# A two-block transformer on one core: moved roundings and taps beside a scan, and cross-attention scores in three rounded passes

## The reference, cut to what matters

```python
def mem_cross_attention(xn, mem, mem_g, wq, wk, wv, wo):   # 4 heads of 256, 512 tokens, 256 memory rows
...
    s = jnp.einsum('bshd,bmhd->bhsm', q, k).astype(jnp.float32) * (XATTN_HEAD_DIM ** -0.5)
    pr = jax.nn.softmax(s, axis=-1).astype(v.dtype)
    o = jnp.einsum('bhsm,bmhd->bshd', pr, v).reshape(B, S, D_MODEL)
    return o @ wo
...
def stick_breaking_attention(q, k, v):      # second block, 8 heads of 64, s < t
        z = jnp.einsum("bqhd,bkhd->bhqk", qb, kb) * scale
        log_beta = jax.nn.log_sigmoid(z)
        log_one_minus = jnp.where(mask, jax.nn.log_sigmoid(-z), 0.0)
        tail = lax.cumsum(log_one_minus, axis=3, reverse=True) - log_one_minus
        weights = jnp.where(mask, jnp.exp(log_beta + tail), 0.0)
...
        c = glu_a * jax.nn.sigmoid(glu_b)
        c = causal_depthwise_conv(c, conv_dw_w[layer], conv_dw_b[layer])   # 31 taps, 512 channels
        c = jax.nn.silu(layer_norm(c, conv_ln_g[layer], conv_ln_b[layer]))
        mixed = jnp.concatenate([attn, c], axis=-1) @ w_out[layer]
```

## Time and profile before

| | us |
|---|---|
| median of 3 runs | 1230.13 (1229.78 to 1230.42) |
| the profiled execution, its own time | 1229.72 |
| its span in the trace | 1227.9 |
| PE busy | 1206.8 |
| PE idle between 686 and 835 us (sum of its six waits there) | 15.6 |

### The profile page before, as it was taken

One profiled execution on the slowest core, in us unless ns is written; L12 is line 12 of the kernel. 1 busy time (PEld: TensorE's weight loads), 2 busy tenths in 40 slices (PEclk: granted clock), 3 DMA queues, 4 the chain that ended last, 5 costly groups with the idle time before them and its releaser, 6 DMA issues.

```text
span 1227.9 us, 16300 instructions
## 1 busy us (share of the span) xinstructions
PE 1206.8 (98%) x5526; PEld 993.2 (81%) x5526; DVE 598.3 (49%) x868; ACT 502.4 (41%) x667; POOL 592.0 (48%) x475
## 2 busy tenths in 40 slices
PE   9999999999999999999999999969999999999998
PEld 7988888888888888888888876648888888888887
DVE  6772435434653165414665899965333223321431
ACT  7432443343443144323464248746433223332331
POOL 5875553233445444463466752324444434444444
PEclk9999999999999999999999999989999999999999
DMA  7444332122333322232233332102232323223222
GB/s 300 138 138 137 103 103 69 52 69 69 103 102 103 104 85 87 102 120 70 80 125 104 103 101 71 35 18 86 86 103 89 116 86 102 95 82 114 81 77 82
DMA packets 34224, 119.46 MB, mean 97 GB/s; under 512 B 4095, under 2 KB 4223, under 8 KB 33919
## 3 DMA queue, kind: packets, MB, share of 16 engines
q1 hardware_dynamic: 33886, 118.53, 28.7%
q10 hardware_dynamic: 288, 0.24, 0.1%
HBM read 115.61 MB, written 2.10 MB: 96 GB/s over the span
## 4 chain that ended last, share of the span: by engine, by line
PE 91%; DVE 7%; ACT 2%; DMA 0%; issue 0%; POOL 0%; DVEq 0%; POOLq 0%; ACTq 0%
PE ps L1271 29%; PE ps L1273 29%; PE ps L1272 29%; DVE slab L1149 3%; DVE ps L1149 2%; PE ps L1438 1%; PE ps L1594 0%; PE ps L1337 0%; DVE slab L1178 0%; PE ps L1624 0%; DVE slab L1212 0%; DVE slab L797 0%; PE ps L1453 0%; PE ps L1412 0%; DMA w_raw<-weights 0%; PE ps L1403 0%
## 5 line engine op out<-in xcount | busy, mean ns | idle before, releaser
L373 POOL TENSOR_TENSOR w_lo<-w_raw,w_hi 128x512 fp32r<-128x512 f32 x430 | 558.5, 1323 | 595.3 <-ACT w_hi L487 356.0
L1271 PE MATMUL ps<-xg_hi,w_hi 128*128 128x512 f32 x960 | 377.1, 393 | 0.6 <-DVE slab L1168 0.6
L1273 PE MATMUL ps<-xg_hi,w_lo 128*128 128x512 f32 x960 | 374.1, 390 | 0.0
L1272 PE MATMUL ps<-xg_lo,w_hi 128*128 128x512 f32 x960 | 374.0, 390 | 0.0
L1271 PE MATMUL ps<-y_hi,w_hi 128*128 128x512 f32 (+1 forms) x608 | 232.4, 382 | 0.0
L1272 PE MATMUL ps<-y_lo,w_hi 128*128 128x512 f32 (+1 forms) x608 | 230.9, 380 | 0.0
L1273 PE MATMUL ps<-y_hi,w_lo 128*128 128x512 f32 (+1 forms) x608 | 230.5, 379 | 0.0
L1271 PEld LDWEIGHTS ps<-xg_hi,w_hi 128*128 128x128 f32 x960 | 180.4, 188 | 38.4 <-issue 1.0
L1272 PEld LDWEIGHTS ps<-xg_lo,w_hi 128*128 128x128 f32 x960 | 180.4, 188 | 37.8 <-issue 1.0
L1273 PEld LDWEIGHTS ps<-xg_hi,w_lo 128*128 128x128 f32 x960 | 180.3, 188 | 37.6
L487 ACT ACTIVATE w_hi<-w_raw 128x1024 fp32r<-128x1024 f32 x124 | 130.4, 1051 | 126.1 <-PE ps L1273 126.1
(11 more groups left out here) (210 smaller groups left out, 1034.0 us busy)
## 6 DMA issues: line engine op xcount, KB each, us to landing
w_raw<-weights SPq DMA_DIRECT2D x199, 512.0 KB, 3.2
w_raw<-weights SPq DMA_DIRECT2D x16, 384.0 KB, 2.9
out_t<-h SPq DMA_DIRECT2D x8, 256.0 KB, 2.0
h<-x_t SPq DMA_DIRECT2D x3, 512.0 KB, 7.9
slab<-mem_t SPq DMA_DIRECT2D x2, 512.0 KB, 10.0
slab<-mats_in SPq DMA_DIRECT2D x1, 1024.0 KB, 5.3
y_free<-slab SPq DMA_DIRECT2D x1, 896.0 KB, 5.4
w_raw<-weights SPq DMA_DIRECT2D x2, 256.0 KB, 3.9
```

The source lines that it names most:

```text
L373: nc.gpsimd.tensor_tensor(w_lo[:, s, half], w_raw[:, s, half], w_hi[:, s, half].bitcast(F32), ALU.subtract).then_inc(done, 1)
L1271: pe.matmul(out, w[0], x[0], start=first, stop=False)
L1272: pe.matmul(out, w[0], x[1], start=False, stop=False)
L1273: return pe.matmul(out, w[1], x[0], start=False, stop=last)
```

## The change

It does two things.

In cross-attention the scores become three passes over rounded queries and keys. ACT rounds each query in its PSUM bank (`x_query_hi`) after DVE has scaled it there, and DVE subtracts (`x_query_lo`), which is what now frees the bank; keys are rounded on ACT and subtracted on DVE once each (`x_keys_hi`, `x_keys_lo`), on DVE ahead of the copy of the spread root. PE's list puts query 6 ahead of the second head's transposes, and cuts the output projection's first two blocks into pieces of two inputs.

In the second mixer ACT's roundings of weight blocks, DVE's taps and four subtractions, and PE's seventh sum change places. The layer norm's squares go in front of the last table change, and their sum moves from POOL to DVE. The number of taps, scans, roundings and table loads stays as it was.

```diff
+        k1_hi = squares_r[:, 0:4 * SEQ].rearrange("p (m t) -> p m t", t=MEM)
+        k1_lo = rounded_units(0, 4).rearrange("p (m t) -> p m t", t=MEM)
...
-            channel_total(1, conv_in, lambda i: pool.wait_ge(ln_square, i + 1))
...
+            def x_keys_hi():
+                act.wait_ge(sums_ready, NORM_XATTN + 1)
+                for n in range(4):
+                    nc.scalar.activation(squares_r[:, n * SEQ:(n + 1) * SEQ], units(n, 1), ACT.Copy).then_inc(x_k_hi, 1)
+
+            def x_query_hi(m):
+                act.wait_ge(x_q_scaled, m + 1)
+                nc.scalar.activation(q1_hi[:, m, :], ps[:, m if m < 4 else m % 2, :], ACT.Copy).then_inc(x_q_hi, 1)
...
             for hd in range(XH):
-                for b in ((4,), (5,), (6, 7), ())[hd]:
-                    weights_hi_for(WQ + b)
+                if hd == 1:
+                    x_query_hi(5)
+                    weights_hi_for(WQ + 5)
+                if hd < 3:
+                    x_query_hi((4, 6, 7)[hd])
                 x_turn_hi(hd)
+                if hd < 3:
+                    weights_hi_for(WQ + (4, 6, 7)[hd])
...
             table(SIGMOIDS)
             s_parts_of(0)
             s_parts_of(1)
             table(LOGS)
             qk_rstd_of(2)
+            weights_hi_for(QK + 1)
+            s_weights(0)
             qk_squares_of(3)
-            weights_hi_for(QK + 3)
-            s_weights(0)
             qk_rstd_of(3)
             s_weights(1)
+            weights_hi_for(QK + 2)
...
-            s_weights(4)
             qk_rstd_of(6)
             qk_rstd_of(7)
+            s_weights(4)
             s_weights(5)
...
             s_weights(6)
+            ln_squares(0, 2)
+            s_weights(7)
+            ln_squares(2, 2)
             table(LOGS)
-            s_weights(7)
-            for i in range(4):
-                act.wait_ge(ln_xc, i + 1)
-                nc.scalar.activation(conv_in[:, i, :], conv[:, i, :], ACT.Square).then_inc(ln_square, 1)
-                if i == 1:
-                    pair_values_hi(3)
+            pair_values_hi(3)
...
             def x_query(m):
-                multiply_by_rstd(q1[:, m, :], WQ + m, m if m < 4 else m % 2).then_inc(banks_freed, 1)
+                bank = m if m < 4 else m % 2
+                multiply_by_rstd(ps[:, bank, :], WQ + m, bank).then_inc(x_q_scaled, 1)
+
+            def x_query_lo(m):
+                dve.wait_ge(x_q_hi, m + 1)
+                nc.vector.tensor_tensor(q1_lo[:, m, :], ps[:, m if m < 4 else m % 2, :], q1_hi[:, m, :].bitcast(F32),
+                                        ALU.subtract).then_inc(banks_freed, 1)
+
+            def x_keys_lo():
+                for n in range(4):
+                    dve.wait_ge(x_k_hi, n + 1)
+                    nc.vector.tensor_tensor(rounded_units(n, 1), units(n, 1), squares_r[:, n * SEQ:(n + 1) * SEQ].bitcast(F32),
+                                            ALU.subtract).then_inc(x_k_lo, 1)
...
+            variance(NORM_XATTN, D)
+            x_keys_lo()
+            spread(NORM_XATTN)
...
-                conv_taps((3, 5, 5, 41)[i])
+                conv_taps((3, 5, 5, 42)[i])
...
+            def ln_square_total():
+                for i in range(1, 4):
+                    dve.wait_ge(ln_square, i + 1)
+                    if i > 1:
+                        dve.wait_ge(ln_added, i + 1)
+                    nc.vector.tensor_tensor(ln_total, conv_in[:, 0, :] if i == 1 else ln_total, conv_in[:, i, :],
+                                            ALU.add).then_inc(ln_added if i < 3 else ln_total_ready, 1)
+
+            def value_steps():
+                dve.wait_ge(v2_shifted, 48)
+                for t in range(ST):
+                    nc.vector.tensor_tensor(v2[:, t, :], v2[:, t, :], v2_before[:, t, :], ALU.subtract).then_inc(v2_steps, 1)
...
+            conv_taps(9)
+
+            s_scan(0)
+            qk_apply(2)
+            qk_input(3)
+            s_scan(1)
+            conv_taps(5)
+            qk_apply(3)
+            conv_taps(1)
+            qk_input(4)
+            value_steps()
+            conv_taps(3)
...
             pair_values_lo(0)
-            conv_taps(5)
+            conv_taps(11)
+            qk_input(6)
...
+                if hd == 0:
+                    pe.wait_ge(x_k_lo, 4)
                 for t in range(ST):
                     for d in range(2):
-                        mm = pe.matmul(ps[:, X_SCORES[hd % 2] + t // 2, (t % 2) * MEM:(t % 2 + 1) * MEM],
-                                       q1[:, 2 * hd + d, t * P:(t + 1) * P], k1[:, 2 * hd + d, :], start=d == 0, stop=d == 1)
+                        tok, m = slice(t * P, (t + 1) * P), 2 * hd + d
+                        mm = three(ps[:, X_SCORES[hd % 2] + t // 2, (t % 2) * MEM:(t % 2 + 1) * MEM],
+                                   (q1_hi[:, m, tok], q1_lo[:, m, tok]), (k1_hi[:, m, :], k1_lo[:, m, :]), d == 0, d == 1)
...
             x_values(0)
             query(5)
+            query(6)
             x_turn(1)
             x_scores_of(2)
             x_values(1)
-            query(6)
             query(7)
             x_turn(2)
+            output(0, (0, 1), begin=True)
             x_scores_of(3)
             x_values(2)
-            output(0, (0, 1, 2, 3), begin=True)
+            output(0, (2, 3))
+            output(1, (0, 1), begin=True)
             x_turn(3)
-            output(1, (0, 1, 2, 3), begin=True)
+            output(1, (2, 3))
             x_values(3)
...
             qk_block(7)
+            qk_sum(6)
             s_turn(4)
-            qk_sum(6)
             qk_sum(7)
```

More of the change, by code:

```diff
@@ L165, in build @@
         y_lo = sb("y_lo", [P, DT, SEQ], F32R)
-        slab = sb("slab", [P, 28 * SEQ])
+        with nc.sbuf_tensor("slab", [P, 28 * SEQ], F32) as slab:
+            pass
+        slab_r = sb("slab_r", [P, 28 * SEQ], F32R)
         memg_hi = y_hi[:, 4:8, :].rearrange("p a (b t) -> p (a b) t", b=2)
@@ L171, in units, with rounded_units @@
             return slab[:, first * SEQ:(first + n) * SEQ]
+        def rounded_units(first, n):
+            return slab_r[:, first * SEQ:(first + n) * SEQ]
         k1 = units(0, 4).rearrange("p (m t) -> p m t", t=MEM)
@@ L223, in build @@
         neg_ones = sb("neg_ones", [P, P])
-        squares = sb("squares", [P, 5 * SEQ])
+        with nc.sbuf_tensor("squares", [P, 5 * SEQ], F32) as squares:
+            pass
+        squares_r = sb("squares_r", [P, 5 * SEQ], F32R)
+        k1_hi = squares_r[:, 0:4 * SEQ].rearrange("p (m t) -> p m t", t=MEM)
+        k1_lo = rounded_units(0, 4).rearrange("p (m t) -> p m t", t=MEM)
         stick_last = squares[:, 2 * SEQ:2 * SEQ + STICK]
@@ L266, in build @@
                                  "x_v_lo"))
+        x_k_hi, x_k_lo, x_q_scaled, x_q_hi = (sem(n) for n in ("x_k_hi", "x_k_lo", "x_q_scaled", "x_q_hi"))
         f_scaled, f_base, f_silu, f_prod = (sem(n) for n in ("f_scaled", "f_base", "f_silu", "f_prod"))
@@ L633, in _ @@
             nc.scalar.preload_act_table_set("natural_log_exp_and_others")
-            for b in range(4):
-                weights_hi_for(WQ + b)
-                if b in (1, 2):
-                    x_values_hi(b - 1)
+            weights_hi_for(WQ)
+            x_keys_hi()
+            x_values_hi(0)
+            x_values_hi(1)
+            weights_hi_for(WQ + 1)
+            x_query_hi(0)
+            x_query_hi(1)
+            weights_hi_for(WQ + 2)
+            x_query_hi(2)
+            weights_hi_for(WQ + 3)
+            x_query_hi(3)
             x_softmax(0)
             for hd in range(XH):
-                for b in ((4,), (5,), (6, 7), ())[hd]:
-                    weights_hi_for(WQ + b)
+                if hd == 1:
[3 more added lines that the diff above has]
+                    x_query_hi((4, 6, 7)[hd])
                 x_turn_hi(hd)
+                if hd < 3:
+                    weights_hi_for(WQ + (4, 6, 7)[hd])
                 if hd + 1 < XH:
@@ L713, in _, with ln_squares @@
             LOGS, SIGMOIDS = "natural_log_exp_and_others", "sigmoid_and_others"
+            def ln_squares(first, n):
+                for i in range(first, first + n):
+                    act.wait_ge(ln_xc, i + 1)
+                    nc.scalar.activation(conv_in[:, i, :], conv[:, i, :], ACT.Square).then_inc(ln_square, 1)
             qk_squares_of(0)
+            qk_rstd_of(0)
             qk_squares_of(1)
-            qk_rstd_of(0)
             weights_hi_for(QK)
             qk_rstd_of(1)
-            weights_hi_for(QK + 1)
             qk_squares_of(2)
-            weights_hi_for(QK + 2)
             table(SIGMOIDS)
@@ L727, in _ @@
             qk_rstd_of(2)
+            weights_hi_for(QK + 1)
+            s_weights(0)
             qk_squares_of(3)
-            weights_hi_for(QK + 3)
-            s_weights(0)
             qk_rstd_of(3)
             s_weights(1)
+            weights_hi_for(QK + 2)
+            table(SIGMOIDS)
             qk_squares_of(4)
-            weights_hi_for(QK + 4)
-            table(SIGMOIDS)
```

(23 more changed lines are left out.)

56 lines of the change are left out of this document (18 added, 38 removed).

## The result

| | before | after |
|---|---|---|
| median of the runs | 1230.28 (1229.78 to 1231.06, 4 runs) | 1210.56 (1210.25 to 1210.83, 4 runs) |
| profiled execution, its own time | 1229.72 | 1210.65 |
| span in the trace | 1227.9 | 1208.9 |

The ratio is 0.9839, 95% interval 0.9822 to 0.9856. Over all runs the executions of the kernel before fall into two groups, one with a mean granted clock of 0.996 (1229.6 to 1230.6 us) and one with 0.993 or 0.994 (1230.9 to 1232.5), those of the kernel after into one (0.999 or 1.000), so a difference of medians holds 0.5 to 1 us that the two profiled executions don't show.

A forecast was written before the change was run, and what follows sets the result against it. PE, busy 98% of the span, was taken to bound the kernel. Second mixer 14.8 (waits 12.3, clock 2.5) plus cross-attention 1.2 makes 16.0 us off 1229.72, 1213.7; with 0.4 for the median 1214.1, range 1211.8 to 1219.5.

The forecast's parts named there:

- 15.6 - 3.3 = 12.3: Second mixer: PE's waits of 15.6 us fall to 3.3 (bounds 2.5 and 8), saving 12.3.
- I count 4 us of excess instead of 12.4: Second mixer, DVE under POOL's residues: excess falls from 12.4 to 4 us (bounds 2 and 12.4), 8.4 off DVE's list.
- The small waits that go upstream: Second mixer, ahead of head 6: small waits vanish, so PE is ready at 799.1 instead of 800.8.
- 7.9 into 1.4: Second mixer, heads 6 and 7: PE's waits for DVE's scans shrink from 7.9 to 1.4 us.
- The 4.0 goes to nothing: Second channel sum: sum of squares ready at 809.0, PE arrives at 810.9, so its 4.0 us wait vanishes.
- Clock, 2.5: Second mixer, behind the 6.7 and 4.0 us gaps: full clock returns, worth 2.5 us (bounds 1.7 and 3.6).
- Cross-attention, 1.2: Cross-attention: scores in 256-wide passes save 1.9 us, two waits cost 0.7, net 1.2 (bounds -2 and 2.3).
- two waits at the last head (0.7): Cross-attention, last head: PE arrives before the probabilities' residues; waits of 0.4 and 0.3 us come to 0.7.
- more than counted: Rival, chance 0.08: the clock gives 3.6 us and the split's waits don't show, time 1211.9.
- collisions only move: Rival, chance 0.12, second mixer: DVE's excess stays near 12.4 us because taps stand everywhere, time 1221.9.
- the splits hold the scores: Rival, chance 0.08: DVE and ACT query steps reach PE 0.8 us late per head; cross-attention loses 2, time 1217.3.
- the weight stream starves: Rival, chance 0.02: later roundings free ring slots later, SP loads later, blocks wait for residues; time 1234.

The follow-up runs named there:

- `fill`: Kernel before plus matmuls of a zero stationary tile in PE's two long gaps, waits for DVE and POOL left: 1227.92 us, ratio 0.9976.
- `dve_order`: Kernel before with only DVE's new list in the second mixer and PE's moved sum: 1226.72 us, ratio 0.9962.
- `thin_before`: Kernel before with POOL's residues of the second mixer's weight blocks cut to 16 columns of each half: 1226.44 us, ratio 0.9966.

## Why the prediction was right and where it failed

The mechanism was right: DVE held by POOL's residues, the scans of head 6, the sum of squares, a clock that comes back. The sizes were short by 3.5 us in all: 2.5 in the second mixer (17.3 for 14.8) and 0.8 in cross-attention (2.0 for 1.2); 0.5 because the 0.4 added for the median did not apply to the kernel after, whose median is 0.1 below its profiled execution; and 0.3 less for a later start. The step that failed is the mixer's count of stalls: 15.6 - 3.3 = 12.3 us of them were to go, 15.2 went (17.3 less 2.1 of clock). It rests on two terms that were mis-sized, the collisions left on DVE (item 1) and the gain upstream (item 2).

1. *"I count 4 us of excess instead of 12.4"*. The excess is 1.6: the taps have none (0.729 against the 0.73 taken as undisturbed) and the value subtractions 4 x (1.07 - 0.68). I placed the residues one by one against a list carried forward from the starts of before, and gave every residue near a tap a collision of one or two instructions; as it came out, only the value subtractions were held. Scan 6 starts at 793.32, which with the 1.73 that came in from ahead is 795.05 in the prediction's count, not 797.3.
2. *"The small waits that go upstream ... bring it to 799.1"*, a gain of 1.7. By the milestones it is 1.45 + 1.70 + 0.99 = 4.1, so that PE arrives at 796.7 in the prediction's count. The wait at head 0's transposes (0.26 and 0.52) had been left among those that remain, and it went; and around it 0.8 more went that the wait view doesn't list.
3. *"7.9 into 1.4"*: into 0.2 by the wait view. By starts the "some 1.1 us in three steps" were nearly right: head 6's ten transposes take 1.96 up to the output matmul, head 7's 1.01, so 0.95 is stall. What was wrong is when: PE leaves them at 796.91 + 1.73 = 798.6 in the prediction's count, not at 799.1 + 1.1 + 1.0 = 801.2. These 2.5 us are the mixer's miss, and they need both, scan 6 2.2 earlier and PE 2.4 earlier. *"The 4.0 goes to nothing"*: right, with 1.0 to spare (the sum ends at 805.23, PE comes at 806.21) instead of 1.9. What stood ahead of ACT's third square was not a residue but the rounding, and with it there the wait stayed 3.96 however early DVE was.
4. *Clock, 2.5*: 2.1 by the milestones, 1.9 to 2.3 by `fill`. Slightly too much.
5. *Cross-attention, 1.2*: 2.0. The 24 passes are 0.12 apart and a head's scores end 2.87 to 3.0 behind their start, as forecast:

```profile
193.15 0.28 PE L1329 MATMUL ps<-squares_r,slab_r 128*128 128x256 f32 x1
193.26 0.28 PE L1330 MATMUL ps<-slab_r 128*128 128x256 f32 x1
...
195.90 0.28 PE L1331 MATMUL ps<-squares_r,slab_r 128*128 128x256 f32 x1
196.02 0.40 PE L1329 MATMUL ps<-xg_hi,w_hi 128*128 128x512 f32 x1
```

   Counted with the transposes ahead, the four heads give 0.58, 0.59, 0.75 and 0.58, 2.5 instead of 1.9. The change from plain to rounded matmuls that I left with heads 1 to 3 shows at head 1 as 0.20 in place of 0.12 for the first pass, but the transposes ahead take 0.79 in place of 0.87. Of the two waits at the last head (0.7) one came, 0.24: the residues were ready 2.7 behind the transposes' start, as worked out, but PE was there after 2.5, not 2.2, since the six matmuls between took 1.64. By the milestones it costs 2.50 - 1.99 = 0.5:

```profile
241.82 1.09 PE L1514 MATMUL ps<-ident,slab 128*128 128x128 f32 x8
...
244.54 0.51 PE L1329 MATMUL ps<-xg_hi,y_hi 128*128 128x512 f32 x1 [0.24 <-DVE xg_lo L1117]
```

6. The range. I set its low end by "more than counted", which moved only the clock and the split's waits. It should have taken in the better bound that I had myself given for the collisions, 2 in place of 4, and for the waits, 2.5 in place of 3.3; 0.8 of waits, 1.1 of clock and 1.1 of cross-attention, the better ends of the bounds, reach 1211.1 already, and the collisions' bound goes further.

Of the rivals, "collisions only move", "the splits hold the scores" and "the weight stream starves" did not happen. The first is what `dve_order` looks like, with taps at 0.93. "More than counted" came nearest with 1211.9, but by a sum that was not it: the clock gave 2.1, not 3.6.

The rule of the Trainium skill (SBUF — State Buffer, "SBUF: two separate sides"), that a DVE instruction with two SBUF inputs and a GpSimd one reading SBUF shut each other out, is borne out by `thin_before` (921 to 727 ns) and by scans with a PSUM operand, whose four pieces take 2.93 to 2.95 us a head in every run, with POOL's residues over them or not.

## What to carry to other kernels

When one engine slows another, taking the collision away frees time only if the victim's own queue has work to put there: move both lists, and count collisions by which instruction lies under which. Read the gain of a wait from the start-to-start distance of the same instruction in both traces, since around short waits the wait view lists only part of the stall. An engine blamed for a late result (POOL's additions) may only pass on the lateness of the one ahead of it (ACT's rounding, which itself waits for PE); a wait that stays the same to 0.01 us in six kernels points to a chain that starts at the engine that waits.
